# Queries and keys of two attentions made feature by feature, with the weights stationary, and rotated across partitions

## The reference, cut to what matters

```python
def apply_rope(x, cos, sin):            # latent tokens only, 64 features of a head
    half = x.shape[-1] // 2
    x1, x2 = x[..., :half], x[..., half:]
    return concatenate([x1 * cs - x2 * sn, x2 * cs + x1 * sn], axis=-1)

dq, dk = h @ w_in[:, 672:1696], h @ w_in[:, 1696:2720]   # 16 maps of 64 features each
sq, sk = h @ w_in[:, 3744:4768], h @ w_in[:, 4768:5024]  # 16 query heads, 4 key heads of 64
s = einsum('...qd,...kd->...qk', q * 64 ** -0.5, k)      # scores, then softmax, then @ v
```

## Time and profile before

| what | value |
|---|---|
| time, median of 3 runs | 2376.84 us (2376.47 to 2377.56) |
| span of the profiled execution | 2374.9 us, 1.9 us below that median; its own time is not listed apart |
| PE busy | 2357.6 us, 99% of the span |
| DVE busy, ACT busy | 1463.9 us (62%), 1176.4 us (50%) |
| PE share of the chain that ended last | 94% |
| mean granted TensorE clock | 0.998 |

### The profile page before, as it was taken

One profiled execution on the slowest core, in us unless ns is written; L12 is line 12 of the kernel. 1 busy time (PEld: TensorE's weight loads), 2 busy tenths in 40 slices (PEclk: granted clock), 3 DMA queues, 4 the chain that ended last, 5 costly groups with the idle time before them and its releaser, 6 DMA issues.

```text
span 2374.9 us, 33590 instructions
## 1 busy us (share of the span) xinstructions
PE 2357.6 (99%) x12849; PEld 1975.0 (83%) x12849; DVE 1463.9 (62%) x2427; ACT 1176.4 (50%) x2137; POOL 137.2 (6%) x219
## 2 busy tenths in 40 slices
PE   8999999999999999999999999999999999999999
PEld 6988888788887888988878878888888888888887
DVE  4565564776657435765547676756689745566565
ACT  5553223753247433664346455564466555645643
POOL 2020000520000000010013000000000000000000
PEclk9999999999999999999999999999999999999999
DMA  8503543134530322426423524665655652655654
GB/s 257 138 19 117 167 147 93 36 117 132 157 101 2 107 83 79 116 89 182 120 80 94 159 85 133 199 193 167 183 165 184 195 179 70 201 177 178 194 169 133
DMA packets 172975, 320.64 MB, mean 135 GB/s; under 512 B 15110, under 2 KB 29568, under 8 KB 172304
## 3 DMA queue, kind: packets, MB, share of 16 engines
q1 hardware_dynamic: 168368, 303.68, 41.5%
q0 software_dynamic: 4448, 14.81, 2.3%
HBM read 313.46 MB, written 3.15 MB: 133 GB/s over the span
## 4 chain that ended last, share of the span: by engine, by line
PE 94%; DVE 3%; ACT 2%; issue 1%; DMA 0%; SPq 0%; POOL 0%; DVEq 0%; ACTq 0%
PE bank L1083 20%; PE bank L1085 20%; PE bank L1084 20%; PE bank L1155 7%; PE bank L1078 4%; PE bank L1080 4%; PE bank L1079 4%; PE bank L1340 3%; PE bank L1363 2%; PE bank L1308 1%; PE bank L1499 1%; PE bank L1311 1%; PE bank L1314 1%; PE bank L1459 1%; DVE w_low_part L2174 1%
## 5 line engine op out<-in xcount | busy, mean ns | idle before, releaser
L2174 DVE TENSOR_TENSOR w_low_part<-w_raw,w_high_part 128x1024 fp32r<-128x1024 f32 (+3 forms) x544 | 638.9, 1187 | 502.6 <-ACT w_high_part L1581 499.5
L1581 ACT ACTIVATE w_high_part<-w_raw 128x1024 fp32r<-128x1024 f32 (+3 forms) x544 | 553.3, 1030 | 689.2 <-PE bank L1085 530.8
L1083 PE MATMUL bank<-w_high_part,h_high 128*128 128x512 f32 (+3 forms) x1888 | 725.6, 384 | 1.7 <-DVE w_low_part L2174 0.6
L1085 PE MATMUL bank<-w_high_part,h_low 128*128 128x512 f32 (+3 forms) x1888 | 717.1, 380 | 0.0
L1084 PE MATMUL bank<-w_low_part,h_high 128*128 128x512 f32 (+3 forms) x1888 | 716.3, 379 | 0.0
L1083 PEld LDWEIGHTS bank<-w_high_part,h_high 128*128 128x128 f32 x1888 | 355.3, 188 | 69.6 <-DVE w_low_part L2174 2.8
L1085 PEld LDWEIGHTS bank<-w_high_part,h_low 128*128 128x128 f32 x1888 | 355.1, 188 | 66.5
L1084 PEld LDWEIGHTS bank<-w_low_part,h_high 128*128 128x128 f32 x1888 | 355.5, 188 | 62.7
L1964 ACT ACTIVATE stage<-bank,neg_max 128x512 f32<-128x512 f32 (+1 forms) x240 | 146.8, 617 | 71.8 <-DVE neg_max L2717 55.7
L1155 PE MATMUL bank<-ident,stage 128*128 128x128 f32 (+1 forms) x1048 | 151.3, 278 | 1.1 <-ACT stage L1964 0.6
L1155 PEld LDWEIGHTS bank<-ident,stage 128*128 128x128 f32 (+1 forms) x1048 | 117.8, 140 | 32.3 <-issue 16.5
(11 more groups left out here) (396 smaller groups left out, 3223.7 us busy)
## 6 DMA issues: line engine op xcount, KB each, us to landing
w_raw<-in_w_in_dram SPq DMA_DIRECT2D x160, 512.0 KB, 3.6
w_raw<-in_a_w_in_dram SPq DMA_DIRECT2D x96, 512.0 KB, 4.2
w_raw<-in_b_w_in_dram SPq DMA_DIRECT2D x80, 512.0 KB, 4.2
w_raw<-in_w_branch_dram SPq DMA_DIRECT2D x48, 512.0 KB, 3.8
w_raw<-in_w_mod_dram SPq DMA_DIRECT2D x37, 512.0 KB, 3.8
w_raw<-in_a_w_out_dram SPq DMA_DIRECT2D x32, 512.0 KB, 4.4
w_raw<-in_c_w_in_dram SPq DMA_DIRECT2D x32, 512.0 KB, 3.8
w_raw<-in_w_out_dram SPq DMA_DIRECT2D x16, 512.0 KB, 3.8
```

Source lines behind the costliest of these rows:

```text
L1083: pe.matmul(o, high, wh, start=(k == 0), stop=False)
L1085: mm = pe.matmul(o, low, wh, start=False, stop=(k == u.kt - 1))
L1581: nc.scalar.activation(WH[:, n % PART_SLOTS, 0:kt, 0:width], raw[:, 0:kt, 0:width], ACT.Copy).then_inc(*S.up("w_high", c))
L2174: v.tensor_tensor(WL[:, s, 0:kt, 0:width], raw[:, 0:kt, 0:width], WH[:, s, 0:kt, 0:width].bitcast(F32), ALU.subtract).then_inc(*S.up("w_lo ...
```

## The change

The seven units of a layer are made feature by feature: a 128x128 block of weights is stationary and the tokens of h stream, 512 of them (256 for the queries of layer 1). A unit of 512 columns has four blocks, `sk` two, each with a bank. So the result is already turned and `turn_qk` goes away for them. The rotation now is across partitions: ACT copies the four 32-partition quarters of a block's latent half to swapped places in `stage` (L1684 after), DVE multiplies by the cosine table (L2324) and the sine table (L2325) and adds (L2326), ACT writes the high part and DVE the low part. The unit's pools alternate: dq 0, dk 0, dv 0, sk and sq 1 take "turn4", the others stay "wide".

```diff
-                pend.append(gemm("rope", (name, l, j), tiles, ("h", l), w_in, D, col + 512 * j, 512, j=j, name=name))
-                if len(pend) > 1:
-                    with_turn(pend.pop(0))
+                gemm("rope", (name, l, j), tiles, ("h", l), w_in, D, col + 512 * j, 512, j=j, name=name,
+                     pool="wide" if j else "turn4")
...
-                 head=(l, 1, qt) if j else None)
-            if pend:
-                with_turn(pend.pop(0))
+                 head=(l, 1, qt) if j else None, pool="wide" if j else "turn4")
...
-        pend = [gemm("swa_k", ("sk", l), ALL_TILES, ("h", l), w_in, D, OFF_SKV, SKV, name="sk")]
+        gemm("rope", ("sk", l), ALL_TILES, ("h", l), w_in, D, OFF_SKV, SKV, j=0, name="sk", pool="turn4")
...
+                 pool="turn4" if j else "wide")
...
+            def gemm_turned(u):
...
+                    for b in range(last + 1):
+                        if n == 0:
+                            open_banks[b] = take(u.more["pool"], (u.key, b))
+                        o = banks[open_banks[b]][:, a:512]
+                        block = slice(P * b, P * b + P)
...
+                            high, low = HH[:, k, a:512], HL[:, k, a:512]
+                            wh, wl = WH[:, slot, kk, block], WL[:, slot, kk, block]
+                            pe.matmul(o, wh, high, start=(k == 0), stop=False)
+                            pe.matmul(o, wh, low, start=False, stop=False)
+                            mm = pe.matmul(o, wl, high, start=False, stop=(k == u.kt - 1))
...
+            def rotate(u):
...
+                        act.wait_ge(*S.filled(key))
+                        if u.tiles[0] in CTX_TILES:
+                            for rows, hi, _ in parted(u, b, False):
+                                nc.scalar.activation(hi, ps(key)[rows, 0:256], ACT.Copy, scale=scale)
...
+                        for q in range(4):
+                            a, other = 32 * q, 32 * (q ^ 1)
+                            last = nc.scalar.copy(swapped[a:a + 32, :], ps(key)[other:other + 32, 256:512])
+                        last.then_inc(*S.up("halves_swapped", key))
+                    if b:
...
+                        act.wait_ge(*S.at("rotated", key))
+                        for rows, hi, _ in parted(u, b - 1, True):
+                            last = nc.scalar.activation(hi, rotated[rows, :], ACT.Copy, scale=scale)
+                        last.then_inc(*S.up("lat_high", key))
...
+                        dve.wait_ge(*S.at("halves_swapped", key))
+                        if u.tiles[0] in CTX_TILES:
+                            part(key, ps(key)[:, 0:256], False)
+                        v.tensor_tensor(rotated, ps(key)[:, 256:512], CSH[:, 0, :], ALU.mult).then_inc(*S.empties(key))
+                        link(v.tensor_tensor(swapped, swapped, CSH[:, 1, :], ALU.mult))
+                        v.tensor_tensor(rotated, rotated, swapped, ALU.add).then_inc(*S.up("rotated", key))
+                    if b:
...
+                        dve.wait_ge(*S.at("lat_high", key))
+                        part(key, rotated, True).then_inc(*S.up("rope_parted", key))
```

More of the change, by code:

```diff
@@ L574, in program @@
         staged = [(s[1], t) for s in steps if s[0] == "gemm" and s[1].kind in
-                  ("mla_q", "rope", "swa_k", "b_qk") for t in s[1].tiles]
+                  ("mla_q", "b_qk") for t in s[1].tiles]
         stage_no = {(u.key, t): n for n, (u, t) in enumerate(staged)}
+        turning = [(u.key, b) for u in units if u.kind == "rope" for b in range(u.width // P)]
+        turning_no = {key: n for n, key in enumerate(turning)}
         busy = [step for step in steps if step[0] not in ("modulation", "small")]
@@ L1066, in gemm @@
                         if n == 0:
-                            open_banks[t] = take("wide", (u.key, t))
+                            open_banks[t] = take(u.more.get("pool", "wide"), (u.key, t))
                         b = open_banks[t]
@@ L1093, in gemm @@
                     turn_qk(turned)
+            def gemm_turned(u):
+                open_banks = {}
+                a = P * u.tiles[0]
+                last = u.width // P - 1
+                for n, (src, k0, kt, col, width) in enumerate(u.chunks):
+                    while late and late[0][0] <= n:
+                        turn(*late.pop(0)[1])
+                    c = u.at[n]
+                    pe.wait_ge(*S.at("w_low", c))
+                    slot = part_of[c] % PART_SLOTS
+                    for b in range(last + 1):
[3 more added lines that the diff above has]
+                        block = slice(P * b, P * b + P)
+                        for kk in range(kt):
+                            k = k0 + kk
+                            for t in u.tiles:
+                                once(left_ready(u.left, k, t))
+                            high, low = HH[:, k, a:512], HL[:, k, a:512]
[3 more added lines that the diff above has]
+                            mm = pe.matmul(o, wl, high, start=False, stop=(k == u.kt - 1))
+                        if n == len(u.chunks) - 1:
+                            mm.then_inc(*fills(open_banks[b]))
+                            if b == last:
+                                S.same("w_used", c, f"bank{open_banks[b]}_filled")
+                        elif b == last:
+                            mm.then_inc(*S.up("w_used", c))
             def keys_and_values(u):
@@ L1929, in turn_piece @@
                     cols = slice(P * t, P * t + P)
[L1930 to L1935, removed]
+                    j = u.more["j"]
+                    nc.scalar.mul(QT[0:MQ, 4 * j:4 * j + 4, cols], src, SCALE[0]).then_inc(*S.empties(key))
             def attend_first(l, r, qt):
@@ L2672, in turn_piece @@
                                     ALU.mult).then_inc(*S.empties(key))
-                if u.kind in ("rope", "swa_k"):
-                    for t in u.tiles[n:n + 1]:
-                        key = ("turn", u.key, t)
-                        hi, lo, scale = parted(u, t)
-                        if u.key[0] == "dq" and u.key[1] == 0:
-                            dve.wait_ge(S.sem("acc_saved"), 16)
-                        low(key, lo, ps(key)[:, :].rearrange("p (n c) -> p n c", n=4), hi, scale=scale)
                 if u.kind != "b_qk":
```

130 lines of the change are left out of this document (65 added, 65 removed).

## The result

The changed kernel took 2395.56 us, median of 4 runs (2395.15 to 2397.64), against 2376.77 us (2376.47 to 2377.56) for the kernel before: 18.8 us more, ratio 1.008, interval 1.0066 to 1.0093. It is 0.8% slower, where the forecast was 2374.1 us.

What follows compares the result with a forecast made beforehand. PE was taken to bound the kernel: turns -19.8, breaks in its stream -1.0, matmuls +1.3, an old wait -0.6, new waits +14.9 make -5.2 us, hence 2371.6; with 2.5 for the clock, 2374.1 us, range 2363 to 2380.

Steps and rivals of the forecast that it cites:

- The turns: PE's transposes of dq, dk, sk and sq in both layers go away: -19.8 us.
- The matmuls: PE's matmuls in both layers: sk saves 0.63 us per layer, four layer-1 units cost 0.63 each; together +1.3 us.
- place (6): Layer 1, sk to sq 0: PE waits 1.4 us for sq 0's fourth weight chunk, prepared only behind the rotation.
- I take 0.26, as nothing in their order makes them wait: ACT's quarter copies in the rotation start 0.26 us apart (bounds 0.26 to 0.40), so DVE at 1.87 us a block paces it.
- rival D: Partition-crossing copies take 0.40 us each and ACT paces the rotation: 2388 with everything, 2382 for half with a fall; chance 0.13.
- (1): Sum after sk, layer 0, wants bank 5, held by block 1's rotation: PE waits 5.3 us.
- (2) and (3): Layer 0: dv 0 waits 3.7 us behind dk 1's sum in bank 4; dk 0 waits 2.4 behind dq 1's in bank 5.
- (4): Sum after sq 1, layer 0, wants block 2's bank 4 until its cosine step ends: PE waits 1.7 us.
- one fall: PE's long stillness brings one fall of the granted clock to half rate: 0 to 5.1 us, taken as 2.5.
- rival B: The clock holds and the waits stay as summed: 2371.6 us; chance 0.22.
- place 5: Layer 0: dq 0 wants the sum's bank while it is still being read; PE waits 0.4 us.
- A: The forecast itself: waits as summed plus one fall of the clock, 2374.1 us, own range 2371 to 2378; chance 0.45.

Runs made afterwards that it cites:

- experiment 4: Kernel before, with one transpose instead of four per turned tile of dq, dk, sk and sq (result incomplete): 2362.05 us.
- experiment 11: Changed kernel with four layer-0 sums in bank 7, layer 1's fourth weight chunk prepared earlier, and DVE reading two sums earlier: 2366.05 us, ratio 0.9955.
- experiment 6: Changed kernel, each of ACT's four quarter copies made on partitions 0 to 31, 64 columns each (result wrong): 2378.80 us.
- experiment 2: Changed kernel with 88 extra unread matmuls of 512 columns filling PE's five long waits: 2385.20 us.
- experiment 1: Changed kernel with the sums before dq 0 and after dq 1, dk 1 and sk of layer 0 moved to bank 7: 2372.28 us, ratio 0.9985.
- experiment 5: Changed kernel, each quarter copy reading the same 32 partitions it writes instead of its neighbour's (result wrong): 2396.87 us.
- experiments 6 to 10: Changed kernel with four 64-column copies on 32 partitions (one start; output, input or both moving) or on all 128: 2378.80 to 2381.72 us.

## Why the prediction was wrong

**What held.** The turns (-19.8 us forecast; 19.2 by experiment 4, 19.1 less busy time in experiment 11). The matmuls: 96 of 256 columns in dq 0 of layer 1 run from 1138.13 to 1149.64, 11.51 us, the distance of the earlier trace rows. All six places and their releasers, and the order of size of the first five; place (6) came out third (4.0 us) instead of fifth. That a long wait brings the clock down.

**The step that failed** is "I take 0.26, as nothing in their order makes them wait", with "so DVE paces it" built on it. The row is of operations that all start at partition 0. The quarter copies each start in another group of 32, and the measured 0.37 lies near the upper end of the bounds, past the 0.30 from which rival D decides against the kernel. The size of D was nearly right place by place: (1) grew by 1.85 us where it said 2.2, (2) and (3) by 1.8 and 1.5 (it said 2.1), (4) by 1.35 (1), (6) by 2.6 (3), and two late chunks made 1.7 of the 6 us. A smaller part is the pieces of 64 partitions of sk, which I took at 0.26 on ACT and 0.34 on DVE and which stand 0.39 and 0.43 apart.

**The second step** is a size: "makes me expect one fall" of the clock, 2.5 us. There were five, 10.4 us. A fall costs about what I took; waits of 3.05, 3.9 and 4.0 us bring one too, and the two errors multiply, since slower copies lengthened exactly the waits that were still short of it (with the short copies of experiment 6 there were three falls). The ground for "one fall", stillness "twice to four times longer than any borne", was read too roughly: PE's list of waits before also has one of 1.3 us (for L2592, at 29 us) and one of 3.4 us at its first instruction, and the fall at the start came with waits of 0.74 us at most between short matmuls. So the start shows no long gap, and can't confirm what the prediction cites from the Trainium skill (TensorE: Matmul & The Clock Gate) on such gaps; the five falls of the changed kernel and experiment 2 do.

**The sum with measured terms**: 2371.6 for rival B, + 25.7 - 14.9 = 10.8 for the waits, + 10.4 for the clock: 2392.8, against 2395.56. Of the 2.8 us missing, 1.2 lie ahead of dq 0 (it starts at 291.99 against 290.38, and 0.4 of that is place 5), in the start-up, where the clock's first fall comes at another moment in each run; the other 1.6 us I didn't locate. For experiment 1 the same sum gives 2371.6 + 10.8 - 14.7 = 2367.7 with no clock; measured 2372.3, so 4.6 us remain for two falls and the start.

**The chances.** The forecast's own reason against itself was "these copies ... not at that pace", at 0.13. The rows for it (either end of 0.26 to 0.40) were in the text; the choice of the lower end took "independent" to mean "overlapping". None of the rows chosen for the forecast has two neighbouring operations with different starting partitions, but the trace before has such pairs. L1681 writes the keys of the first attention in two pieces, which read partitions 0 to 63 and then 64 to 127 of a bank. Timeline of ACT, kernel before, then the line's group (busy us, mean ns of one, idle before):

```profile
69.56 1.20 ACT L1681 ACTIVATE k_high<-bank 64x512 fp32r<-64x512 f32 x2 [0.17 <-PE bank L1110]
```

```profile
L1681 ACT ACTIVATE k_high<-bank 64x512 fp32r<-64x512 f32 x16 | 9.4, 589 | 1.1 <-PE bank L1110 1.0
```

Two of 0.59 us take 1.20 us: they start 0.61 us apart, end to end, and nothing in their order makes the second wait. The same shows on DVE (L2272, two of 0.69 us take 1.39). These rows don't say why, but they speak for the upper bound, and with them D had a better claim than A's 0.26. D with everything, 2388, and five falls are 2398; the range ended at 2380.

**Why a large saving came out as a loss.** Nothing of it was lost where it was made. 25.7 us of PE's time went to waiting for banks and chunks that the rotation held, 10.4 us more to half rate behind these waits; 19.8 us of transposes can't pay for that. With the banks sorted out, the saving appears (experiment 11).

## What to carry to other kernels

Before costing operations on parts of the partitions, see where each starts: here neighbours with different 32-partition starts ran end to end, on ACT and on DVE, so four quarter copies were four full durations. The trace of the kernel before can hold such a pair; look for it. When work moves from PE to ACT and DVE behind a unit, look for whoever wants the banks or buffers it holds, tiny steps above all: eight matmuls of one column that take a bank in turn held up a whole engine for 7 us, and one other bank brought back 23 us. Add something for the clock to a long wait on PE: here those of 3 us or more cost some 2 us each on top, and shorter ones sometimes brought a fall too.

## What was not expected of the hardware

- ACT's copies overlap by some 0.1 us when they start at the same partition, on 32 partitions as on 128, and not at all when input or output starts in another group of 32: 0.11 against 0.21 to 0.22 us apart at 64 columns, 0.26 against 0.37 at 256. Crossing from one group to another costs nothing in itself (1.49 us for four, crossed or straight).
- In the changed kernel the granted clock fell around every wait of 3.0 us or more (3.05, 3.9, 4.0, 5.5, 7.15); the waits of 2.8 and 2.9 us that stayed with the short copies brought one each; filler matmuls in these waits kept it at 1.00 and returned 10.4 us.
- Length of the wait alone doesn't decide it: waits of 1.0 to 1.3 us at the sum after sq 1 brought a fall in three executions and none in another, one of 0.4 us at the sum before dq 0 brought one in experiment 5, and waits of 1.3 to 1.6 us at dk 0 brought none in experiments 6 to 10. Why is open.
